# Sixteen experts' weights through five buffers in the order of use, and an activation formed ahead of the additions

## The reference, cut to what matters

```
logits = h @ router_w + router_b
top_v, top_i = lax.top_k(logits, TOP_K)          # 4 of 32
gates = jax.nn.softmax(top_v, axis=-1)
...
def expert_block(args):
    xe, e = args
    hc = xe @ w1[e] + b1[e]                      # w1[e]: 1024 x 2048
    hg = jnp.minimum(hc[:, :D_FF], SWIGLU_LIMIT)
    hl = jnp.clip(hc[:, D_FF:], -SWIGLU_LIMIT, SWIGLU_LIMIT)
    act = hg * jax.nn.sigmoid(SWIGLU_ALPHA * hg) * (hl + 1.0)
    return act @ w2[e] + b2[e]                   # w2[e]: 1024 x 1024
...
x = x + sum over the four experts of gate * expert(h)
```

## Time and profile before

| | us |
|---|---|
| runs (3): lowest, median, highest | 1583.81, 1588.65, 1589.62 |
| the profiled execution, its own time | 1586.84 |
| span of its trace, first to last instruction | 1585.1 |
| mean granted TensorE clock | 0.967 |
| PE busy | 1467.3 (93% of the span) |
| PEld busy | 743.8 (47%) |
| DVE busy | 500.9 (32%) |
| ACT busy | 217.3 (14%) |
| POOL busy | 60.6 (4%) |

### The profile page before, as it was taken

One profiled execution on the slowest core, in us unless ns is written; L12 is line 12 of the kernel. 1 busy time (PEld: TensorE's weight loads), 2 busy tenths in 40 slices (PEclk: granted clock), 3 DMA queues, 4 the chain that ended last, 5 costly groups with the idle time before them and its releaser, 6 DMA issues.

```text
span 1585.1 us, 23037 instructions
## 1 busy us (share of the span) xinstructions
PE 1467.3 (93%) x9751; PEld 743.8 (47%) x9751; DVE 500.9 (32%) x992; ACT 217.3 (14%) x498; POOL 60.6 (4%) x103
## 2 busy tenths in 40 slices
PE   5999878798799998999999999999999999999897
PEld 4776666698647745433333333333333333333222
DVE  2484514423510503313223132232222322322313
ACT  2333201231002403000000000000000000000001
POOL 3010100230000000000000000000000000000000
PEclk9999989899898996999999999999999999999999
DMA  6332263100526766599999999999999999999992
GB/s 166 97 107 80 66 166 104 45 4 10 177 118 239 293 255 283 223 428 430 426 433 427 425 433 429 426 434 425 428 431 429 425 431 429 427 432 427 427 383 91
DMA packets 74693, 471.92 MB, mean 298 GB/s; under 512 B 14660, under 2 KB 48155, under 8 KB 58080
## 3 DMA queue, kind: packets, MB, share of 16 engines
q1 hardware_dynamic: 73804, 469.68, 72.5%
q10 hardware_dynamic: 788, 0.78, 0.2%
HBM read 463.40 MB, written 7.05 MB: 297 GB/s over the span
## 4 chain that ended last, share of the span: by engine, by line
PE 31%; DMA 29%; DVE 1%; issue 0%; ACT 0%; SPq 0%; DVEq 0%; ACTq 0%
DMA w<-in_w_e_dram 29%; PE ps L2639 12%; PE ps L2676 11%; PE ps L2448 2%; PE ps L2615 2%; PE ps L2631 1%; PE ps L2452 1%; PE ps L2662 1%; PE ps L2609 1%; PE ps L2667 0%; PE ps L2597 0%; PE ps L2588 0%; DVE x L2832 0%; PE ps L2750 0%; PE ps L2600 0%
## 5 line engine op out<-in xcount | busy, mean ns | idle before, releaser
L2676 PE MATMUL ps<-w,kvb 128*64 128x512 f32 x1024 | 233.8, 604 | 17.3 <-DMA w<-in_w_e_dram 17.3
L2848 DVE TENSOR_SCALAR kvb<-ps 128x512 f32<-128x512 f32 x32 | 22.1, 692 | 619.2 <-PE ps L2639 619.2
L2676 PEld LDWEIGHTS ps<-w,kvb 128*64 128x64 f32 x1024 | 69.7, 138 | 159.2 <-issue 123.6
L521 PE MATMUL ps<-yT,wst 128*128 128x288 f32 (+1 forms) x496 | 126.1, 413 | 0.0
L2639 PE MATMUL ps<-wa,kvb 128*64 128x512 f32 x512 | 113.4, 595 | 0.0
L2639 PE MATMUL ps<-wc,kvb 128*64 128x512 f32 x512 | 113.4, 595 | 0.0
L2639 PE MATMUL ps<-wb,kvb 128*64 128x512 f32 x512 | 112.6, 592 | 0.0
L2639 PE MATMUL ps<-wd,kvb 128*64 128x512 f32 x512 | 112.6, 592 | 0.0
L521 PEld LDWEIGHTS ps<-yT,wst 128*128 128x128 f32 (+1 forms) x496 | 93.2, 190 | 30.2 <-issue 5.2
L2832 DVE TENSOR_TENSOR x<-x,ps 128x1024 f32<-128x1024 f32 x66 | 80.2, 1216 | 34.2 <-PE ps L2615 34.1
L2799 ACT ACTIVATE kvb<-kvb 128x512 f32<-128x512 f32 x32 | 20.2, 630 | 487.0 <-DVE kvb L2848 487.0
(11 more groups left out here) (626 smaller groups left out, 1526.0 us busy)
## 6 DMA issues: line engine op xcount, KB each, us to landing
w<-in_w_e_dram SPq DMA_DIRECT2D x64, 2048.0 KB, 25.4
wb<-in_w_e_dram SPq DMA_DIRECT2D x16, 4096.0 KB, 29.7
wc<-in_w_e_dram SPq DMA_DIRECT2D x16, 4096.0 KB, 27.1
wd<-in_w_e_dram SPq DMA_DIRECT2D x16, 4096.0 KB, 29.9
wa<-in_w_e_dram SPq DMA_DIRECT2D x16, 4096.0 KB, 26.9
wst<-in_w_in_dram SPq DMA_DIRECT2D x15, 1024.0 KB, 5.7
kvc<-in_cache_mem_k_dram SPq DMA_DIRECT2D x5, 1024.0 KB, 9.2
kvc<-in_cache_mem_v_dram SPq DMA_DIRECT2D x5, 1024.0 KB, 6.7
```

The costliest lines, as they stand in the source:

```text
L521: ins = nc.tensor.matmul(ps[:q.n, 6 + t % 2, 0:T], wst[:, q.group % NG, c, q.at:q.at + q.n], hT[:, c, :], start=(c == 0), stop=(c == KC - 1))
L2676: ins = nc.tensor.matmul(ps[CAP * half:CAP * half + CAP, 2, :], actT[:, c, h, :], w2[:, h, c, 512 * half:512 * half + 512], start=(h == 0 ...
L2848: nc.vector.tensor_scalar(hg[:, :], ps[:, 0, :], LIMIT, None, ALU.min).then_inc(hg_ok, 1)
```

## The change

On SyncE's queue, for the last sixteen items (16 to 31, t from 0 to 15), the buffers lose their fixed meaning. The weights are counted as units of 4 MiB in the order in which TensorE uses them: unit 3t is half 0 of w1 of item 16 + t, unit 3t + 1 is half 1, unit 3t + 2 is w2. Unit u lies in buffer u mod 5 of the list wa, wb, w2, wc, wd. Within item 16 + t are issued: w2 of the next item once the first half of w1 is used (`w1_half`), b1 and half 0 of w1 of the item after that once the second half is used (`w1_done`; b1 itself isn't behind it), and half 1 of w1 once w2 is used (`w2_done`). The first 16 items are as before, and the sixteenth's successor finds its weights where they were. On VectorE, in the last four items, the addition of `combine(0)` stands behind the two products of the activation, and no more ahead of them.

```
+        def landed(more, u):
+            first = sum(1 for v in range(5, u + 1) if v % 5 == u % 5)
+            second = sum(1 for v in range(5, u + 1) if v % 5 == u % 5 and v % 3 == 2)
+            if u % 5 == 2:
+                return 128 * more + 144 + 16 * first, 128 * more + 144 + 16 * second
+            return 64 * more + 80 + 16 * first, 16 * second
@@ SyncE
-                    for s in range(15):
-                        if s < 14:
-                            next_w1(8 * more + 8 + s, s)
-                        next_w2(8 * more + 8 + s)
+                    for t in range(15):
+                        k = 8 * more + 8 + t
+                        e = expert(k + 1)
+                        sp.wait_ge(w1_half, k + 1)
+                        for h in range(2):
+                            sp.dma_start(as_w2(3 * t + 5)[:, h].unsqueeze(1), w2_d[h][:, e]).then_inc(
+                                (slot_in, half_in)[h][(3 * t + 5) % 5], 16)
+                        if t < 14:
+                            e = expert(k + 2)
+                            load_b1(sp, e, t % 2)
+                            for h in range(2):
+                                u = 3 * t + 6 + h
+                                sp.wait_ge((w1_done, w2_done)[h], k + 1)
+                                sp.dma_start(as_w1(u).unsqueeze(1), w1_d[h][:, e]).then_inc(slot_in[u % 5], 16)
@@ TensorE
-                    for s in range(8):
-                        item(more, 1, s, True)
-                    for s in range(8):
-                        item(more, 2, s, s < 4)
+                    for t in range(16):
+                        item(more, 1 + t // 8, t % 8, t < 12, 3 * t)
@@ VectorE, item
-                        dve.wait_ge(cmb_done, 3 * k + 1)
-                        add(0, 6)
+                        if more_x:
+                            dve.wait_ge(cmb_done, 3 * k + 1)
+                            add(0, 6)
                         dve.wait_ge(th_ok, k + 1)
                         nc.vector.scalar_tensor_tensor(hg[:, :], th[:, :], 1.0, hg[:, :], ALU.add, ALU.mult).then_inc(
                             glu_ok, 1)
                         dve.wait_ge(glu_ok, k + 1)
                         nc.vector.scalar_tensor_tensor(hl[:, :], hl[:, :], 1.0, hg[:, :], ALU.add, ALU.mult).then_inc(
                             act_ok, 1)
+                        if not more_x:
+                            dve.wait_ge(cmb_done, 3 * k + 1)
+                            add(0, 6)
```

More of the change, by code:

```diff
@@ L2409, in experts @@
         y = sb(st, "y", [P, 512])
+        slots = [w.rearrange("p c n -> p (c n)") for w in (w1[0] + [w2[:, :, :, :].rearrange("p h c n -> p (h c) n")] + w1[1])]
+        slot_in = [*ahead.w1_in, w2_in[0], *ahead.w1_in1]
+        half_in = [sem(f"half_in{u}") for u in range(2)] + [w2_in[1]] + [sem(f"half_in{u}") for u in range(3, 5)]
         b1_in = [sem(f"b1_in{s}") for s in range(2)]
@@ L2431, in experts, with as_w1, as_w2 @@
         last_bank = (6, 4, 0)
+        def as_w1(u):
+            return slots[u % 5].rearrange("p (c n) -> p c n", c=HK)
+        def as_w2(u):
+            return slots[u % 5].rearrange("p (h c n) -> p h c n", h=2, c=HK)
+        def landed(more, u):
[4 more added lines that the diff above has]
+            return 64 * more + 80 + 16 * first, 16 * second
         def expert_x(s):
@@ L2616, in combine, with item @@
                         ins.then_inc(cmb_done, 1)
-                    def item(j, o, s, more_x):
+                    def item(j, o, s, more_x, u=None):
                         k, first = 8 * j + 8 * o + s, o == 0 and s == 0
-                        xe, w, p = expert_x(s), w1[s % 2], 4 * o + s // 2
+                        xe, p = expert_x(s), 4 * o + s // 2
+                        if u is None:
+                            wu, wd = w1[s % 2], w2
+                            w1_ok = [(sem, 64 * j + 16 * p + 16) for sem in w1_in[s % 2]]
+                            w2_ok = [(sem, 16 * k + 16) for sem in w2_in]
+                        else:
+                            wu, wd = [as_w1(u), as_w1(u + 1)], as_w2(u + 2)
+                            w1_ok = [(slot_in[(u + h) % 5], landed(j, u + h)[0]) for h in range(2)]
+                            w2_ok = [((slot_in, half_in)[h][(u + 2) % 5], landed(j, u + 2)[h]) for h in range(2)]
                         if s % 4 == 0:
@@ L2633, in item @@
                         for h in range(2):
-                            pe.wait_ge(w1_in[s % 2][h], 64 * j + 16 * p + 16)
+                            pe.wait_ge(*w1_ok[h])
                             for c in range(HK):
@@ L2639, in item @@
                                         ins = nc.tensor.matmul(ps[CAP * half:CAP * half + CAP, g, :], xe[:, h, c, :],
-                                                               w[h][:, c, c0:c0 + 512], start=False,
+                                                               wu[h][:, c, c0:c0 + 512], start=False,
                                                                stop=(h == 1 and c == HK - 1))
@@ L2672, in item @@
                         for h in range(2):
-                            pe.wait_ge(w2_in[h], 16 * k + 16)
+                            pe.wait_ge(*w2_ok[h])
                             for c in range(HK):
@@ L2676, in item @@
                                     ins = nc.tensor.matmul(ps[CAP * half:CAP * half + CAP, 2, :], actT[:, c, h, :],
-                                                           w2[:, h, c, 512 * half:512 * half + 512],
+                                                           wd[:, h, c, 512 * half:512 * half + 512],
                                                            start=(h == 0 and c == 0), stop=(h == 1 and c == HK - 1))
```

## The result

| | before | with the change |
|---|---|---|
| runs, median (lowest to highest), us | 1588.65 (1582.66 to 1590.34, 5 runs) | 1576.97 (1572.21 to 1578.40, 5 runs) |
| profiled execution, own time / span | 1586.84 / 1585.1 | 1572.76 / 1571.0 |
| granted TensorE clock | 0.967 | 0.968 |

The ratio is 0.9928 with a 95% interval of 0.9898 to 0.9957, so 0.4 to 1.0% faster. The medians are 11.7 us apart, the spans of the two traces 14.1. Forecast were 1576.3 and a difference of 12.4.

The account below looks back on a forecast made before the run. The weight stream was taken to bound the kernel, with TensorE's 32.8 us behind the last long wait at its end; 11.5 us (loads) plus 0.9 (activation), 12.4 off the median 1588.65, gave 1576.3 us, range 1571 to 1583.

Parts of the forecast that it names:

- the loads' term: End of the kernel: loading weights in order of use leaves less work behind the last long wait, saving 11.5 us.
- The landing that counts: Half 1 of w1 of expert 31 would land at 1539.4 us, where w2 of expert 30 had landed before.
- The uncertain term: At that landing, early DMA engines going on with w2 of 31 might move it 3 us either way; taken as nothing.
- the rule on engines 7 and 15: Skill page's rule that these DMA engines are usually slower; they would be late in either order, leaving 12.4 us.
- Rival 1: Engine skew makes w1 of expert 31 land 5 us later: gain 7.4 us, kernel 1581.3 us; chance 0.09.
- rival 2: Landings of experts 17 to 31: stream slows, at 409 GB/s to 1597 us; chance 0.04 slower, 0.03 lesser fall within 0.5%.
- The activation's term: Expert 31, between w1 and w2: the addition leaves the place ahead of the activation's products, saving 0.9 us.
- TensorE catches up: At 28.27 us per expert from expert 16, TensorE reaches half 1 of w1 of expert 31 at 1534.2, 5 us to spare.
- Waits: TensorE's waits for w2 vanish from about expert 17, returning for half 1 of w1 from about 27, under 2 us each.
- rival 3: At the switch of order the stream runs dry, a pause of some 4 us, so 1580 us; chance 0.02.
- any window under 420 GB/s: Sign that the prediction is wrong: any window from 1130 to 1540 us with a stream rate under 420 GB/s.
- always the second half of w2: Experts' stage before the change: claimed that TensorE's waits for w2 always end with its second half landing, 29.47 us per expert.

Follow-up runs that it names:

- second set of runs: The unaltered changed kernel measured once more, on one chip beside two kernels with split w1 loads: median 1573.00 us, 0.9911 of the kernel before.
- activation only: Kernel before with only the activation moved ahead of the addition in the last four experts, loads in the old order: 1582.16 us, ratio 0.9968.
- last 2: Changed kernel with the new order of loads starting at expert 30 instead of 16: 1585.91 us, 0.9988 of the kernel before.
- run of three parts: Changed kernel with each half of w1 in the new order loaded in three DMAs (half, quarter, quarter): 1574.36 us, 0.9927 of the kernel before.
- run of two parts: Changed kernel with each half of w1 in the new order loaded in two DMAs of 2 MiB: 1571.04 us, 0.9905 of the kernel before.
- split at the end: Changed kernel with only half 1 of w1 of experts 29, 30 and 31 loaded in two DMAs: 1569.14 us, 0.9905 of the kernel before.

## Why the prediction was right

The mechanism held, and the loads' term came out as worked out. That the median came within 0.7 us of the forecast is in part luck: by the traces the two tails differ by 14.0 us and not by 12.4, and the medians tell the difference only to within 6.8 to 16.2. The second set of runs has the medians 14.3 apart. By its steps:

- **The landing that counts** was put at 1539.4 and came at 1539.32. From the first load it is 969.8, 970.3 and 970.1 for w2 of expert 30 (before, activation only, last 2) and 969.9 to 971.2 for half 1 of w1 of expert 31, in the eight traces in which TensorE waited for a landing of the old sizes. The uncertain term, whether the DMA engines that finish early would take rate from the last ones by going on, was put at zero within -3 and +3. It is zero within the 1.4 us by which the landings differ: with nothing behind it the landing came at 971.2 too. Which DMA engines are the late ones no view of the traces shows, so the rule on engines 7 and 15 that the prediction quotes is untested here. The Trainium skill (DMA: Bandwidth & Descriptors, Latency and other measured facts) calls its best guess at the cause specific to DMAs by way of GpSimd, and these are SyncE's. Rival 1 is out, and so is rival 2, a slower stream, for transfers of the change's sizes (429 GB/s). It is true for smaller ones (426 and 424).
- **The loads' term**, 11.5 us, measured 11.4 by itself.
- **The activation's term** was mis-sized: 0.9 was forecast and it is 2.5 alone (30.3 against 32.8), 2.5 on top of the loads too (18.9 against 21.4). The step that failed is "0.87 are in w2's 7.89 already and could be saved", which I left out of the sum, and that the two small groups of matmuls ahead of w2 had been drawn out by 0.8 in the same way I hadn't seen at all. The 0.94 of the addition were right. The rest, 1.6 us, is TensorE's clock, which in every trace stays up through these groups when the wait for VectorE is 0.99 us, and at 1.93 in some experts only. The Trainium skill (TensorE: Matmul & The Clock Gate, Why this matters for your kernels) ties the clock to gaps between bursts of matmuls. The runs agree in the direction. They don't agree in the length: losses stand here behind waits of 1.93 and even 1.26 us, shorter than the gaps of that page, and none behind one of 2.81 (last section).
- **TensorE catches up** was right, with more room than stated. It was to reach half 1 of w1 of expert 31 at 1534.2 if never made to wait. I had left out that the last experts have no gather and, with the change, a shorter chain: 26.6 us each in place of 28.3. So eight experts in the new order are enough where my rate of 28.27 would have left TensorE 4.7 us late (1544.1 against 1539.4). With four it comes 4 to 5 us late (975.2 against 970 to 971).
- **Waits** for half 1 of w1 "by under 2 us each" was too low: they begin at expert 27 as forecast (0.15, then 0.76), but then come 2.41 at 1479.80 and 2.42 at 1509.05, the second with the clock at half speed behind it (8.63 us for the half). Off the path as it happened, since 1.89 us of wait were still left in expert 31.
- **Switching the order** drained nothing; rival 3 is out. From 1130 to 1540 the DMA share is 1.00 and the rate 429 GB/s.
- **Signs that were put badly.** The share was to stay at 1.00 until about 1549. It falls from about 1540 on (0.85, 0.77, 0.52 in windows of 2 us from 1540, 1542 and 1544): the skew of the engines has moved with the last load and isn't gone. And "any window under 420 GB/s" has no length. Over 30 us no window from 1130 to 1520 is under 423, but over 10 us the change has one of 411, and the kernel before, too. Nor is it "always the second half of w2" that a wait ends before: at 1504.95 the whole w2 follows.
- The sum of the parts is 14.0 by the traces (11.46 + 2.52), and 14.1 is the difference of the spans, in which the first load's 1.5 us and the landing's 1.4 cancel. The measured medians are 11.7 apart. From the first load to y the gain is 12.6 us by this trace and 13.8 by the second of the change. Within the interval of the ratio, 6.8 to 16.2 us, all of these fit.

## What to carry to other kernels

In a kernel bound by a stream of weights, as this one, the order of the loads gains at the end of the stream and not while it runs: order them as they are used, and ask what work stands behind the last landing, and behind the last but one. The gain can be worked out from one trace as the difference of two tails, but the consumer has to have caught up by then; how many stages that takes is its lateness divided by the difference of the two paces. When one tail has been shortened, the next bound can be just one unit of the stream away, as here, and each new wait has to be checked for what it does to TensorE's clock.

## What the runs showed of the hardware

- The rate of the stream falls over its last 7 us or so (320, 328, 172, 139 GB/s before; 328, 262, 115, 16 in the run without the last load), so the 16 DMA engines don't end it together. What is left last isn't faster when the rest is idle: 971.2 us to the landing both with and without 4.19 MB behind it, at 16 GB/s in total just ahead of it, one trace each.
- The same bytes in more DMAs come more slowly: 429 GB/s in transfers of 4 MiB (w1) and 2 MiB (w2), 426 with all of 2 MiB, 424 with w1 in 2 and 1 MiB, the last two from one trace each. An issue of a weight load takes 0.33 to 0.37 us in the change and stood for up to 5.3 us in the run of three parts. In the run of two parts those of w1 stood for 1.3 us at most, and the stream was slower all the same. What makes an issue stand, and whether it is the cause of the lower rate, wasn't tried.
- Waits of TensorE and what the next w1 half took: 1.89 us, 7.09; 2.41, 7.09; 2.42, 8.63; 2.62, 8.78; but 2.81 us, 7.09 (in three parts), and in the second run of the change 2.06, 8.78 and 2.41, 8.78. The shortest with a loss is 1.26, 8.78 (split at the end). Length alone doesn't decide. What does was not tried.
- The stretch from the first load to the landing that counts repeats within 1.4 us over those eight traces (969.8 to 971.2), while the issue of that first load itself moved between 566.4 and 576.2 us over all fourteen. So in the traces the spread lies ahead of the experts.
